# Sparse attention core of a hybrid decoder step: another order of the query tiles, and an earlier softmax of the sampled tokens

## The reference

```python
def sparse_attend(q, k_sel, v_sel, valid):
    B, Q = q.shape[:2]
    qg = q.reshape(B, Q, N_KV_HEADS, N_HEADS // N_KV_HEADS, HEAD_DIM)
    s = jnp.einsum('bqgrd,bqkgd->bqgrk', qg, k_sel).astype(jnp.float32) * (HEAD_DIM ** -0.5)
    s = jnp.where(valid[:, :, None, None, :], s, -jnp.inf)
    p = jax.nn.softmax(s, axis=-1).astype(v_sel.dtype)
    o = jnp.einsum('bqgrk,bqkgd->bqgrd', p, v_sel)
    return o.reshape(B, Q, Q_DIM)
...
        sc = indexer_scores(qib, wib, ki, pos[None], k_pos)
        _, idx = lax.top_k(sc, topk)
```

## Time and profile before

| | |
|---|---|
| median of 3 runs | 2657.9 us (2656.54 to 2661.39) |
| the profiled execution | 2655.82 us, of which the span is 2654.0 us |
| core loop, from the first `meta_qk` to the end of the last `spread_scale` | 652.90 to 840.42 us of the span |
| TensorE busy over the span | 2483.8 us (94%) |
| VectorE, ScalarE, GpSimd busy | 1302.9, 746.3, 783.8 us |
| TensorE's granted clock over the span | 0.946 of full speed |

### The profile page before, as it was taken

The page is one execution under the profiler, slowest core; times in us unless marked ns, Lnnn a source line. Parts: engine busy times, 40 slices in busy tenths (PEclk is TensorE's granted clock), DMA queues, the critical chain, the costliest instruction groups (busy, mean ns, idle before and its releaser), DMA issues.

```text
span 2654.0 us, 48017 instructions
## 1 busy us (share of the span) xinstructions
PE 2483.8 (94%) x19652; PEld 2334.6 (88%) x19652; DVE 1302.9 (49%) x1776; ACT 746.3 (28%) x1100; POOL 783.8 (30%) x467
## 2 busy tenths in 40 slices
PE   8999999996699999999999999999979639999999
PEld 8999999753467999999999999999968339999999
DVE  5333355766753533334533334677568742533333
ACT  4121232221243222212322222334566221322122
POOL 3311341242002433034432034202643343331130
PEclk9999999995589999999999999999989659999999
DMA  4223223244022222222222222423440002222312
GB/s 154 103 84 120 78 100 110 96 143 161 1 107 101 80 95 75 99 95 69 105 82 84 103 79 72 144 87 119 182 176 2 32 14 97 80 91 83 108 70 93
DMA packets 61002, 250.55 MB, mean 94 GB/s; under 512 B 9376, under 2 KB 25888, under 8 KB 41056
## 3 DMA queue, kind: packets, MB, share of 16 engines
q1 hardware_dynamic: 56672, 223.94, 23.9%
q0 software_dynamic: 4224, 25.17, 2.7%
HBM read 233.58 MB, written 15.49 MB: 94 GB/s over the span
## 4 chain that ended last, share of the span: by engine, by line
PE 87%; POOL 4%; DVE 4%; issue 3%; ACT 2%; DMA 0%; DVEq 0%; POOLq 0%; ACTq 0%
PE acc L598 46%; PE acc L628 22%; PE acc L753 4%; PE acc L1063 1%; PE acc L1999 1%; PE acc L911 1%; PE acc L1084 1%; POOL xT L2419 1%; PE acc L821 1%; PE acc L2046 1%; PE acc L1072 1%; PE acc L1052 1%; PE acc L2039 1%; POOL wl L2410 1%; POOL yl L2494 1%
## 5 line engine op out<-in xcount | busy, mean ns | idle before, releaser
L598 PE MATMUL acc<-xh,wh 128*128 128x268 f32 (+1 forms) x3344 | 685.1, 286 | 20.0 <-DVE xl L410 16.2
L598 PE MATMUL acc<-xl,wh 128*128 128x268 f32 (+1 forms) x3344 | 685.2, 286 | 0.0
L598 PE MATMUL acc<-xh,wl 128*128 128x268 f32 (+1 forms) x3344 | 682.8, 285 | 0.0
L598 PEld LDWEIGHTS acc<-xh,wh 128*128 128x128 f32 x3344 | 520.6, 189 | 21.0 <-issue 16.0
L401 DVE TENSOR_TENSOR wl<-raw,wh 128x2048 fp32r<-128x2048 f32 x185 | 430.6, 2328 | 205.7 <-ACT wh L342 205.7
L598 PEld LDWEIGHTS acc<-xh,wl 128*128 128x128 f32 x3344 | 521.6, 189 | 0.0
L598 PEld LDWEIGHTS acc<-xl,wh 128*128 128x128 f32 x3344 | 520.8, 189 | 0.0
L342 ACT ACTIVATE wh<-raw 128x2048 fp32r<-128x2048 f32 x194 | 370.3, 1909 | 506.2 <-PE acc L628 410.5
L553 POOL TENSOR_TENSOR gh<-scr,ones 128x536 f32 (+1 forms) x88 | 94.5, 1074 | 949.3 <-DVE scr L430 949.3
L423 DVE TENSOR_TENSOR scr<-acc,rstd 128x536 f32<-128x536 f32 (+1 forms) x88 | 62.7, 712 | 514.7 <-PE acc L598 514.6
L628 PE MATMUL acc<-gh,wh 128*128 128x268 f32 (+1 forms) x1408 | 287.7, 286 | 0.9 <-POOL gl L554 0.9
(11 more groups left out here) (423 smaller groups left out, 2992.9 us busy)
## 6 DMA issues: line engine op xcount, KB each, us to landing
raw<-in_w_ffn_in SPq DMA_DIRECT2D x88, 1024.0 KB, 4.8
raw<-in_w_ffn_out SPq DMA_DIRECT2D x32, 768.0 KB, 4.1
raw<-in_w_ssd_in SPq DMA_DIRECT2D x21, 1024.0 KB, 4.7
raw<-in_w_ffn_out SPq DMA_DIRECT2D x32, 640.0 KB, 3.8
raw<-in_w_attn_in SPq DMA_DIRECT2D x9, 1024.0 KB, 4.8
kic<-in_kpages SPq DMA_DIRECT2D x64, 128.0 KB
xT<-in_state_ssm SPq DMA_DIRECT2D x8, 1024.0 KB, 6.8
out_hs<-xT SPq DMA_DIRECT2D x8, 1024.0 KB, 5.0
```

What stands on the lines that cost most here:

```text
L598: mm = nc.tensor.matmul(acc[:, slot * 4 + 2 * t + h, 0:(N - lo) // 2], w[:, slot, c:c + P], x[:, kt, half_of(lo, h)], start=(kt == 0 and w ...
```

## The change

Three things are edited.

1. `PACKS` lists the tiles in the order 3, 2, 4, 1 instead of 1, 2, 3, 4. Pairs 0 to 7 now have 384 keys (128 before), pairs 8 to 15 have 256 as before, pairs 16 to 23 have 512 (384 before), pairs 24 to 31 have 128 (512 before).
2. The six VectorE steps of the sampled softmax follow each other in steps 10 to 15; its exponential moves from step 15 to 13. TensorE's four parts move from the ends of steps 11, 13, 15, 17 to those of 10, 11, 12, 14.
3. `VALUES` falls from 18 to 16, so that the sampled tokens' values run in steps 16 to 30 and the joins in 17 to 31.

```diff
-    PACKS = [(j, a) for j, _, _ in QTILES for a in range(2)]
+    PACKS = [(j, a) for j in (3, 2, 4, 1) for a in range(2)]
...
-    VALUES = SIDE + 8
+    VALUES = SIDE + 6
...
-            if n % 2 == 1 and SIDE < n < SIDE + 8:
-                sample_steps((n - SIDE) // 2)
+            if n - SIDE in (0, 1, 2, 4):
+                sample_steps((0, 1, 2, 4).index(n - SIDE))
...
-            if n == SIDE + 5:
+            if n == SIDE + 3:
                 act.wait_ge(sexp_asked, S)
                 nc.scalar.activation(Ss[:], Ss[:], ACT.Exp, scale=QSCALE).then_inc(sexp_done, 1)
...
-        SAMPLE_STEPS = {SIDE + n: step_of for n, step_of in ((0, sample_threshold), (1, sample_mask), (3, sample_max),
-                                                            (4, sample_less_max), (6, sample_sum), (7, sample_scale))}
+        SAMPLE_STEPS = {SIDE + n: step_of for n, step_of in ((0, sample_threshold), (1, sample_mask), (2, sample_max),
+                                                            (3, sample_less_max), (4, sample_sum), (5, sample_scale))}
```

## The result

| | before | changed |
|---|---|---|
| median | 2657.35 us (2656.54 to 2661.39, 4 runs) | 2673.15 us (2669.68 to 2676.25, 4 runs) |
| profiled execution, span | 2655.82, 2654.0 us | 2674.28, 2672.5 us |
| granted clock over the span | 0.946 | 0.943 |

The ratio is 1.0059, 95% interval [1.0046, 1.0071]: 15.8 us slower. The forecast was 2669 us, 11 to 12 us slower.

A forecast was written before the change was run, and what follows sets the result against it. Bounds by stretch: latency in A, TensorE and VectorE taking turns in B, full TensorE in C. +10 + 15.3 - 13.2 = +12.1 us on 2655.8 gave 2667.9, median 2669; range 2656 to 2680.

The forecast's parts named there:

- the prediction's chain: Mask's end to pair 16: TensorE and VectorE wait in turn; pair 16 starts at 30.7 us at the lower clock.
- the bare sum: Sampled softmax: VectorE's sum, 3.85 us, for which TensorE's L1040 waits, idle 4 to 5 us.
- A: Loop start to pair 10, 57.95 us before: 384-key pairs cost +10 us, bounds -0.5 and +16.
- The rival of a clock that stays low through the bisection: In the loop up to pair 10: clock stays low, +16 us there, total +18, 2675 us; chance 0.14.
- one that rises with the first wide pairs: Rival: clock rises early and holds; A -0.5, B +10.7, C -13.2, median 2655 us; chance 0.15.
- B: Pair 10 to pair 18, the six sampled steps: 38.7 us against 23.4 after the mask, +15.3, bounds +10.7 and +21.
- the waiting transpose: L1034 before pair 12's scores: TensorE pulls nothing past it; by the opposite rule B would lose 5 us of its 15.
- C: Pair 18 to the loop's end, TensorE full: narrow pairs last give -13.2 us, bounds -17 and -9.
- the low stretches: Low clock behind `meta_qk` from pair 18 on: 8% of the clock, some 6 us, left unchanged.

The follow-up runs named there:

- experiment 5: Changed kernel with the transpose of the maxima (L1034) moved behind pair 12's scores and the sum's product (L1040) behind pair 15's; 1.0027 of the kernel before.
- Experiment 1: Kernel before with only the new tile order 3, 2, 4, 1, softmax and values where they stood; 0.9996 of the kernel before.
- experiment 3: Changed kernel with only the transpose of the sampled maxima (L1034) moved behind pair 12's `meta_qk` and scores; 1.0032 of the kernel before.
- Experiment 10: Kernel before with new tile order, sampled mask in two halves, and three unread filler matmuls in each of pairs 0 to 4; 2651.35 us, 0.9978.
- 4: Changed kernel with only TensorE's product of the sampled sums (L1040) moved behind pair 15's scores; 1.0045 of the kernel before.
- 6: Changed kernel with the sampled tokens' values starting from pair 18 again, as before; 1.0035 of the kernel before.
- 12: Kernel before with the new tile order and the sampled mask in two halves, without filler matmuls; 1.0 of the kernel before.

## Why the prediction was right, and where its sizes were off

**The direction and the mechanism** held: slower, by a chain of hand-overs between TensorE and VectorE in the six sampled steps. Of the 14.7 to 15.9 us that the stretch from the mask to pair 16 lost, experiment 5 gives 6.5 to the two places where TensorE stands in front of scores; the prediction's chain holds the bare sum and the low clock behind it too, but no run separates those. What was to be seen was seen: TensorE idle 10.02 us before L1034, VectorE idle 4.33 behind L1648, a second wait of 5.00 before L1040, pair 10 at 719.9 (forecast 720), pair 18 at 778.7 (776), the loop's end at 857.1 (852), no wait of TensorE for values.

**A: +10 forecast, +8.05 measured.** VectorE works 42.60 us instead of 36.96 and TensorE 49.20 instead of 39.14. VectorE's 5.6 us are more than the 4.3 of the prediction, which counts the masking alone: the copies of the turned tiles (L1707) also went from 0.28 to 0.55 us each in eight pairs, and the sum put them at nothing without a reason. The clock rose in pair 5, as forecast, fell to 0.5 behind the `meta_qk` of pair 8, as forecast, but was back before pair 10:

```profile
704.87:707.87 3.00, 2.28 (x24) 1.98 (x24) 1.90 (x8) 0.88 (x4) 0.00 (x0) 1.00 0.00 0
707.87:710.87 3.00, 2.89 (x18) 2.67 (x17) 0.18 (x1) 0.00 (x0) 0.00 (x0) 0.60 0.00 0
710.87:713.87 3.00, 2.78 (x12) 1.73 (x12) 2.10 (x11) 1.28 (x5) 0.00 (x0) 0.50 0.00 0
...
716.87:719.87 3.00, 1.78 (x29) 1.60 (x29) 2.73 (x14) 1.19 (x5) 0.00 (x0) 1.00 0.02 5
```

A term to within 2 us was more than the matter allows. Seven executions with the new order and equal instructions up to pair 10 took 63.68, 63.70, 66.00, 66.25, 66.47, 66.49 and 68.22 us, mean 65.8; three with the old order 57.93, 57.93 and 57.95. So the order costs A 7.9 us on average, and forecast and measured value agree within this spread. In the three with the old order the clock stays at 0.50 all through A. The rival of a clock that stays low through the bisection asked for +16, and the rival of one that rises with the first wide pairs for -0.5; 68.2 and 63.7 are far from both, so neither happened in any of the seven.

**B: +15.3 forecast, +18.4 measured.** This is the mis-sized term. The chain worked out at the lower clock was right at every link. Counted from the end of the mask at 736.42: pair 12's scores end at 5.6 us (forecast 5.5), pair 13's at 10.1 (10.1), the subtraction at 14.7 (15.0), the exponential at 16.8 (17.1), the sum at 20.6 (20.9), pair 16 starts at 30.5 (30.7). What failed was the step behind it, that the upper clock would take part of the chain back: "With the upper clock wherever TensorE has worked for a while it starts at 25. I take 28." The upper clock did come, for the scores at 749.86, but TensorE was about to run dry there, so it saved nothing, and behind the 5.00 us of waiting the clock was low again, when the 9.9 us of work up to pair 16 stood on the path. It held on through pair 16's scores (2.08 us) and into the first token's values (2.93 us where 1.93 stood), so that pairs 16 and 17 took 11.8 us instead of 10.7. In this chain the full clock sat where it was worth nothing. Of the 3.1 us, 2.5 are this step, 1.1 pairs 16 and 17, and the way to the mask's end gave back 0.5 (16.55 us where 17.0 were forecast). Experiment 1 shows the same stretches without the six-step softmax: 15.76 and 9.03 us.

That the waiting transpose lets nothing pass was a premise here. The trace shows the work behind it begin at 736.88, right at its end. The Trainium skill (TensorE: Matmul & The Clock Gate, Part 2), by which matmuls keep the program's order, is borne out by that, and by experiment 3, where the same work, written ahead of it, ran ahead of it.

**C: -13.2 forecast, -10.8 measured.** The work was counted rightly and the clock too high. I left the low stretches "as they are". The changed kernel's clock over C is 0.87 against 0.92. At two levels of 0.5 and 1, that is 2 x 0.13 x 78.35 = 20.4 us at the lower one against 2 x 0.08 x 89.15 = 14.3, and half of such time is loss: 10.2 against 7.1, 3.1 us more. This covers the 2.4 that are missing. Experiment 10, with a clock of 0.91, shows the term without it: its C is 78.81 us and holds one more token's values, 2.9 us by the prediction's estimate, than the changed kernel's; 78.81 - 2.9 - 89.15 = -13.2. How low the clock is over C is itself a draw: the changed kernel and experiments 3, 4 and 5 have equal instructions there and took 78.35, 78.26, 76.80 and 79.77 us at 0.87, 0.87, 0.89 and 0.85. One of the low stretches of the changed kernel in its widest pairs, and one in its narrow pairs:

```profile
788.72:793.72 5.00, 4.88 (x24) 3.53 (x24) 0.58 (x2) 0.00 (x0) 0.00 (x0) 0.67 0.55 233
...
833.72:838.72 5.00, 4.88 (x27) 3.87 (x27) 1.75 (x8) 0.78 (x4) 0.00 (x0) 0.60 0.81 342
```

A `meta_qk` stands in each. TensorE shows 4.88 us busy of 5, and the clock falls all the same. The old order has such stretches too, at its own `meta_qk`; how long each lasts differs from kernel to kernel (0.84 to 0.94 over C in the fourteen), and I found no rule for it.

**Outside the loop** I had nothing, and the two executions differ by 2.8 us. Six executions in which the program took 2652 to 2675 us start the loop at 652.86 to 654.78 us with equal instructions ahead of it, and need 1813.3 to 1815.8 us from its end to the end of the span with equal instructions behind it, so this is their scatter and no effect of the change.

**The sum** for the loop was +12.1 us and is +15.7: B 3.1 and C 2.4 us too low, A 2 too high. That A's error has the other sign is luck, since it lies within the spread of equal executions, and it hides part of the other two, which both come mostly from a clock taken too high. The median came out 4 us above the 2669 forecast.

## What to carry to other kernels

When a side chain is squeezed into fewer steps, count each hand-over's wait on both engines: TensorE's queue stops at the first instruction that waits, so put the waiting one behind the work that is ready (6.5 us here for two of them, with a third left), and still expect the bare length of the long reductions. Work out such a chain at the lower clock: here the stretch in which the clock was up had slack. And an edit that is even by itself, such as the order of the tiles, may be worth keeping beside another: together with the halved mask and the fillers it was 0.2% faster, though which of them it needs is open.

## What the runs showed of the hardware that was not expected

Equal instructions get different clocks. Up to pair 10, seven executions of the same instructions spread over 4.5 us (63.7 to 68.2), with a first, short rise of the clock 24 to 27 us into the loop in five of them and none before 39 us in two. Two pairs of them (experiments 1 and 6, 5 and 12) agree to 0.02 us in length and to 0.01 in the clock of every 3 us, though each pair ran two kernels on two chips. What picks the course no run shows. Where a stretch hovers between the levels, one profile is not enough to size a term of 2 us.

Fifteen further matmuls took the mean clock in A from 0.50 to 0.65 and its length from 57.95 to 56.20 us: the higher clock was worth little where VectorE sets the pace. In C the fourteen kernels lie between 0.84 and 0.94 with TensorE full in all of them, and four with equal instructions there between 0.85 and 0.89.
